# A two-stream transformer kernel: low-rank rows made and turned as two items, and smaller gates for a stage's last eight experts

## What is computed

```python
def _mla_kv(ckv, kr, lp, ang):            # keys and values through a rank of 128
    kv = _rmsnorm(ckv, lp["kv_norm_g"]) @ lp["w_ukv"]
    ...
def _mla_q(cq, lp, ang):                  # queries through a rank of 256
    q = _rmsnorm(cq, lp["q_norm_g"]) @ lp["w_uq"]
    ...
def _peer(h, w_pq, peer_keys, peer_down, peer_up):
    # 8 heads x top 16 of 128x128 experts: 128 experts for each token
    ...
    a = einsum("tkd,td->tk", peer_down[ee], hh)
    act = gg * gelu(a)
    return einsum("tk,tkd->td", act, peer_up[ee])
for l in range(DEPTH):
    m_x = _modulation(c, w_mod[l], b_mod[l])
    mix_x, _ = _token_mix(modulated(x), lp, ang, kv_c)
    x = x + m_x[2] * mix_x
    x = x + m_x[5] * _peer(modulated(x), ...)
    # in layer 0 the same for the context; in layer 1 only its keys and values
```

## Time and profile before

| what | us |
| --- | --- |
| median of three runs | 4265.7 |
| lowest and highest | 4264.2, 4265.86 |
| the profiled execution | 4267.86 |
| its span in the trace | 4266.6 |

### The profile page before, as it was taken

One profiled execution on the slowest core, in us unless ns is written; L12 is line 12 of the kernel. 1 busy time (PEld: TensorE's weight loads), 2 busy tenths in 40 slices (PEclk: granted clock), 3 DMA queues, 4 the chain that ended last, 5 costly groups with the idle time before them and its releaser, 6 DMA issues. The chain is left out here.

```text
span 4266.6 us, 41116 instructions
## 1 busy us (share of the span) xinstructions
PE 3701.3 (87%) x14648; PEld 2615.9 (61%) x14648; DVE 2319.3 (54%) x5440; ACT 658.8 (15%) x1794; POOL 1307.3 (31%) x1125
## 2 busy tenths in 40 slices
PE   8988899998998689999988998767778899878777
PEld 6667787886857578888846884333334787333332
DVE  3331011457658766766752126767774123877774
ACT  2232100110001220000002111111112211111111
POOL 1000000000755446665630003434442001544442
PEclk9999999999999889999999999988999999999989
DMA  8652344433998779999961349979996326999997
GB/s 321 237 202 106 117 151 155 153 117 136 413 383 305 263 255 381 406 399 385 409 247 51 143 167 364 414 311 380 409 412 283 109 105 249 402 419 420 419 414 320
DMA packets 207819, 1208.67 MB, mean 283 GB/s; under 512 B 23696, under 2 KB 24848, under 8 KB 96000
## 3 DMA queue, kind: packets, MB, share of 16 engines
q0 software_dynamic: 154368, 855.71, 50.1%
q1 hardware_dynamic: 53248, 350.32, 21.6%
HBM read 1204.79 MB, written 1.15 MB: 283 GB/s over the span
## 5 line engine op out<-in xcount | busy, mean ns | idle before, releaser
L1222 PE MATMUL bank<-big 128*128 128x256 f32 (+3 forms) x9848 | 2142.1, 378 | 65.4 <-issue 16.8
L1222 PEld LDWEIGHTS bank<-big 128*128 128x128 f32 x9848 | 1834.9, 191 | 375.1 <-issue 85.0
L2406 POOL DMA_INDIRECT big<-in_pboth,big x1024 | 1240.6, 1211 | 1243.0 <-PE bank L1609 651.3
L1609 PE MATMUL bank<-big 128*128 128x512 f32 x2048 | 1009.4, 651 | 304.2 <-ACT big L2370 304.1
L2087 DVE CUSTOM_DVE_ANT_0 big<-big 128x1024 f32<-128x1024 f32 x768 | 926.5, 1223 | 346.8 <-DMA big<-in_pboth,big 336.1
L1609 PEld LDWEIGHTS bank<-big 128*128 128x128 f32 x2048 | 416.4, 208 | 894.3 <-issue 500.0
L2393 POOL TENSOR_TENSOR big<-big 128x1 f32<-128x1 f32 (+1 forms) x49 | 40.9, 834 | 1553.7 <-DVE big L1663 1553.6
L2098 DVE SCALAR_TENSOR_TENSOR big<-big 128x1024 f32<-128x1024 f32 x254 | 326.1, 1284 | 34.8 <-DMA big<-in_pboth,big 11.9
L2370 ACT ACTIVATE big<-big 128x128 f32<-128x128 f32 x512 | 164.7, 391 | 258.6 <-DVE big L2066 251.9
L1257 PE MATMUL bank<-big 128*128 128x128 f32 x596 | 95.9, 297 | 74.2 <-ACT big L2172 23.6
L2360 ACT ACTIVATE big<-big 128x4 f32<-128x4 f32 x128 | 26.4, 206 | 785.3 <-DVE big L2062 785.3
(11 more groups left out here) (203 smaller groups left out, 2191.2 us busy)
## 6 DMA issues: line engine op xcount, KB each, us to landing
big<-in_w SPq DMA_DIRECT2D x104, 1024.0 KB
big<-in_wmod POOLq DMA_DIRECT2D x48, 1024.0 KB, 8.4
big<-in_wgu SPq DMA_DIRECT2D x44, 1024.0 KB
big<-in_wzg SPq DMA_DIRECT2D x36, 1024.0 KB, 4.8
big<-in_wro SPq DMA_DIRECT2D x32, 1024.0 KB
big<-in_wpq SPq DMA_DIRECT2D x24, 1024.0 KB, 4.9
big<-in_wd SPq DMA_DIRECT2D x22, 1024.0 KB
big<-in_pboth,big POOLq DMA_INDIRECT x1024, 18.5
```

The source lines that it names most:

```text
L1222: last = pe.matmul(o, a, b, start=(i == 0), stop=(i == n - 1))
L1609: last = pe.matmul(u.ap, d.ap, row[:, 512 * i:512 * i + 512], start=(k == 0), stop=(k == 127))
L2406: g.indirect_dma_start(out=s.ap, out_offset=None, in_=table, in_offset=bass.IndirectOffsetOnAxis(ap=index, axis=0)).then_inc(s.full[0], 16)
```

## The change

Three edits. First, `low_rank` becomes two items: `low_rank` (product, squares, root) and `low_turn` (turning and taking from PSUM). `mixer` now emits the product of keys and values with the rope key, then the product of the queries, then the turning and `kv_up` of the keys, then the turning and `q_up` of the queries. Loads follow in the order `wkv`, `wcq`, `wukv`, `wuq`. Second, the eight matmuls of `keep_busy` in front of each turning of the x stream are gone. Third, the gates of the last eight experts of a stage (second block of tokens, experts 120 to 127) hold 2, 2, 2, 1 and 1 experts where they held 4 and 4. With the first edit the yields change: `keys_values` hands back 6, 1 and 6 units where it handed 7 and 7, the queries' product 7 and their turning 2 where there was none, so that a mixer's stream stands 8 units later from there on, the context's too; and the side generator takes three steps for keys and values in place of two.

```diff
-    def low_rank(self, banks, sm, ws, wt, hT, ready, n, tmp, dst, gcols):
+    def low_rank(self, banks, sm, ws, wt, hT, ready, n, tmp):
         u = banks.take()
         r = self.rstd(sm, 2, 1.0 / n, EPS)
+        scaled = [self.tick("lowrank_rows"), u.free]
+        self.put("low_rank", ws=ws, wt=wt, hT=hT, ready=ready, n=n, u=u, tmp=tmp, r=r, scaled=scaled)
+        return u.full, scaled
+
+    def low_turn(self, banks, sm, n, tmp, dst, gcols, scaled):
         parts = [banks.take() for _ in range(2)]
-                 warm=8 if sm is self.small else 0,
-                 scaled=[self.tick("lowrank_rows"), u.free])
-        return parts[1]
+        self.put("low_turn", n=n, tmp=tmp, dst=dst, gcols=gcols, parts=parts, scaled=scaled)
+        return parts[1].free
...
-        low = self.low_rank(banks, sm, [w], wt, hT, hT_ok, P, ckn, ckvT, self.col[l, "kvg"])
+        _, scaled = self.low_rank(banks, sm, [w], wt, hT, hT_ok, P, ckn)
...
-        yield
+        yield 6
+        turned = self.low_turn(banks, sm, P, ckn, ckvT, self.col[l, "kvg"], scaled)
+        yield 1
         w = self.load(wr, t["wukv"][l], 1024)
...
-        yield
+        yield 6
         return [r, ku[3].free, vu[1].free]
...
-        kv_ok = yield from self.keys_values(banks, wr, sm, ar, l, hT, hT_ok, K, Vv, cs)
-        if rope_on and l == 1:
-            kv_ok += self.ctx_kv_ok
+        kv = self.keys_values(banks, wr, sm, ar, l, hT, hT_ok, K, Vv, cs)
+        yield next(kv)
...
+        made, scaled = self.low_rank(banks, sm, [w], w.ap.rearrange("p (k n) -> p k n", k=8), hT, None, 256, cqn)
+        w.free(made)
+        yield
+        kv_ok = yield from kv
+        if rope_on and l == 1:
+            kv_ok += self.ctx_kv_ok
+        turned = self.low_turn(banks, sm, 256, cqn, cqT, self.col[l, "qg"], scaled)
+        yield 2
         w = self.load(wr, t["wuq"][l], 1536)
...
+        ends = {(tt, k) for tt, k in steps if k % 4 == 3} | {(1, k) for k in (121, 125, 126)}
+        at = 0
         for n, (tt, k) in enumerate(steps):
...
-            if k % 4 == 3:
+            if (tt, k) in ends:
...
-                a, c = act[:, tt, k - 3:k + 1], 4 * (n // 4 % 8)
-                args = dict(at=a, u=gl[:, c:c + 4], ag=ag[:, c:c + 4], tanh=tick("gelu_tanh"))
-                put("gelu", gat=gat[:, tt, k - 3:k + 1], cubed=tick("gelu_cubed"), **args)
+                m = len(batch)
+                at = 0 if at + m > 32 else at
+                mine = slice(k + 1 - m, k + 1)
+                args = dict(at=act[:, tt, mine], u=gl[:, at:at + m], ag=ag[:, at:at + m], tanh=tick("gelu_tanh"))
+                put("gelu", gat=gat[:, tt, mine], cubed=tick("gelu_cubed"), **args)
+                at += m
...
-            if tt == 0:
-                keep_busy(v, warm)
```

More of the change, by code:

```diff
@@ L779, in keys_values @@
         w.free(vu[1].full)
-        put("kv_up", ws=[w], ckvT=ckvT, K=K, Vv=Vv, ku=ku, vu=vu, ready=low.free)
-        yield
+        put("kv_up", ws=[w], ckvT=ckvT, K=K, Vv=Vv, ku=ku, vu=vu, ready=turned)
+        yield 6
         return [r, ku[3].free, vu[1].free]
@@ L818, in mixer @@
             q_ok = tick("q_turned") if rope_on else u.free
-            put("q_up", ws=[w] if h == 0 else [], w_ok=w.full, wq=wq, cqT=cqT, Q=Q[:, h:h + 2, :], h=h, u=u, ready=low.free,
+            put("q_up", ws=[w] if h == 0 else [], w_ok=w.full, wq=wq, cqT=cqT, Q=Q[:, h:h + 2, :], h=h, u=u, ready=turned,
                 u2=banks.take() if rope_on else None, cs=cs, rt=rt, done=q_ok)
@@ L1451, in col_turn, with low_rank @@
             turn(u, [h[:, (4 * g + i) * P:(4 * g + i + 1) * P] for i in range(4)]).then_inc(u.full[0], 1)
-    def low_rank(ws, wt, hT, ready, n, u, tmp, parts, scaled, warm, **_):
+    def low_rank(ws, wt, hT, ready, n, u, **_):
         opened(u)
@@ L1458, in low_rank, with low_turn @@
         tokens_first(pe, u, wt, hT, n=n).then_inc(u.full[0], 1)
+    def low_turn(n, tmp, parts, scaled, **_):
         for tt, v in enumerate(parts):
             opened(v)
-            if tt == 0:
-                keep_busy(v, warm)
             pe.wait_ge(*scaled[tt])
@@ L1618, in tensor_program @@
                  branch_gate=branch_gate, branch_out=branch_out, mix_out=mix_out, ffn_in=ffn_in, ffn_out=ffn_out, ffn_last=ffn_last, mod=mod,
-                 mod_columns=mod_columns, col_turn=col_turn, low_rank=low_rank, key_rope=key_rope, key_roped=key_roped, kv_up=kv_up, q_up=q_up,
-                 att_score=att_score, att_turnp=att_turnp, att_out=att_out, att_turn=att_turn, fourier=fourier, pool=pool,
+                 mod_columns=mod_columns, col_turn=col_turn, low_rank=low_rank, low_turn=low_turn, key_rope=key_rope, key_roped=key_roped,
+                 kv_up=kv_up, q_up=q_up, att_score=att_score, att_turnp=att_turnp, att_out=att_out, att_turn=att_turn, fourier=fourier, pool=pool,
                  token_gate=token_gate, mix=mix, token_out=token_out, peer_q=peer_q, peer_scores=peer_scores, up_pe=up_pe)
@@ L1900, in col_turn, with low_rank, low_turn @@
         i.then_inc(u.free[0], 1)
-    def low_rank(n, dst, gcols, r, parts, **_):
+    def low_rank(r, **_):
         spread(r)
+    def low_turn(n, dst, gcols, parts, **_):
         for tt, u in enumerate(parts):
@@ L2134, in vector_program @@
                  context_in=context_in, mod_add=mod_add, mod_gain=mod_gain, mod_row=mod_row, mod_zero=mod_zero,
[L2135 removed]
+                 mod_columns=mod_columns, row_scale_v=row_scale_v, col_turn=col_turn, low_rank=low_rank, low_turn=low_turn, key_roped=key_roped, kv_up=kv_up,
                  q_up=q_up, load_cs=load_cs, att_score=att_score, fourier=fourier, pool=pool, mix=mix, token_out=token_out,
```

5 lines of the change are left out of this document (removed).

## The result

The changed kernel took 4254.42 us in the median of 13 runs (4245.61 to 4262.41); the kernel before, run beside it, 4264.43 (4257.22 to 4271.8). The ratio is 0.9975 with a 95% interval of 0.9965 to 0.9984: 10.0 us faster, between 7 and 15. The prediction was -18.3 us, that is 4247.4, and a range from 4237 to 4260: the direction holds and the time lies in the range, but only somewhat more than half of the forecast size came. The profiled executions differ by less, 4267.86 before and 4262.41 after, since the latter is one of the slowest of its 13; so the places are compared by their own lengths, and with the traces of the experiments as repetitions.

What follows compares the result with a forecast made beforehand. PE, busy 87% of the span, was taken as the main bound, with gathers, hand-overs and DVE limiting places. Terms -9.6 + 0.8 - 6.8 - 7.1 + 3.4 + 2 - 1 + 0 = -18.3 gave 4247.4 us, range 4237 to 4260.

Steps and rivals of the forecast that it cites:

- The low-rank part of x: Keys' product to first `q_up` in x's mixers: 29.44 us falls to 24.66, -4.8 per layer, -9.6 for both.
- +0.8 for the clock: Layer 0's keys' product: a slower PE start after slightly longer idle time without the removed matmuls, +0.8 us.
- The clock, rival (c): x's low-rank parts: without the removed matmuls PE stays at 1.2 GHz, work doubles, +42 us, 4289 us; chance 0.04.
- Stage ends: Last experts of both stages: smaller gates let PE finish 3.4 us earlier per stage, -6.8 for both.
- The load queue: End of the context's mixer: PE's 8.22 us wait at 739.28 for a `w1` chunk falls to about 1.1, -7.1.
- Junction: Streams' junction at 2206: more context work on DVE delays the row for `peer_add`, net +3.4 us, bounds +1 to +6.
- Ranking: Merge of x's first mixer output with the context's ranking, 940 to 1031: more DVE instructions, +2 us, bounds -5 to +4.
- The context's low-rank part: Context's mixer: waits covered, but taking the keys falls behind the first block's decays on DVE; -1 us, bounds -4 to +3.
- Side generator: Context's keys and values among layer 0's experts: stalls move, copies' stall 10 to 13 us; 0 taken, bounds -5 to +7.
- Rival (a): The `w1` wait at 739 stays or comes back: sum -11.2, 4254.5 us; chance 0.18.
- Rival (b): Shifted context stream gives more back, junction +6, ranking +4, side generator +7: -6.7, 4259 us; chance 0.15.

Runs made afterwards that it cites:

- e2: The full change with the last experts' gates back at 4 and 4, so the low-rank edits and removed matmuls alone: 4261.86 us, ratio 0.9986 to the kernel before.
- e3: The full change with fewer units handed back, so the two streams merge as before, without the shift: 4255.4 us, ratio 0.9975 to the kernel before.
- e1: The kernel before with only the smaller gates (2, 2, 2, 1, 1) for a stage's last eight experts: 4260.42 us, ratio 0.9987 to the kernel before.
- e6: The kernel before with only gates of 4, 2, 1, 1 for a stage's last eight experts: 4262.74 us, ratio 0.9996 to the kernel before.
- e7: The kernel before with only the eight `keep_busy` matmuls before each turning taken out: 4268.43 us, ratio 1.0009 to the kernel before.
- e4: The full change with the eight `keep_busy` matmuls kept before the first turning of each rank in x: 4264.81 us, ratio 0.9996 to the kernel before.
- e9: The kernel before with only the context's stream moved by 8 units, the shift alone: 4269.62 us, ratio 1.0007 to the kernel before.
- e5: The kernel before with only the loads of `iota` and keys put one `w1` chunk later in SP's list: 4254.09 us, ratio 0.9973 to the kernel before.
- e8: The kernel before with x's new order without `keep_busy`, context keys before queries unshifted, late `iota` and keys loads, gates 2, 2, 1, 1, 1, 1: 4245.08 us, ratio 0.9956.

## Why the prediction was right, and where its size was off

The time lies in the range and the direction held. Of the forecast's -18.3 us some 8 did not come: mostly the two streams, for which the sum of the load queue, the junction, the ranking and the context's part was -2.7 and which gave +2 to +6 up to x's modulated rows at 2230, and partly the stage ends. By the steps of the prediction:

- **The low-rank part of x** (-9.6, with +0.8 for the clock: -8.8). Right, and a little too small: about 6.8 in layer 0 and 3.8 in layer 1, 10.6 us together by e2, e3 and the full change against the five kernels in the old order. In layer 0 the two profiled executions give 4.7 us up to `q_up` (30.81 and 26.08), as forecast; the further 2 us were not in the sum. The granted clock of that whole part was 0.94 before and 0.95 after (0.95 in e1 too), so the +0.8 for a slower start isn't seen there; in layer 1 it went from 0.99 to 0.98. The waits that come back were foreseen with their places. Layer 1's shortfall (-3.4 to `q_up` in the two profiled executions instead of -4.8) is the slower clock in the two first products; in e1 and e6, where the keys' product of the old order met the same clock, the old stretch was 1.6 us longer too, and the difference is 5.0.
- **The clock, rival (c).** It didn't decide, but its mechanism is real and was shown in e7: without the matmuls and without the new order the part gets 5.4 us slower. I had them down as filler on the path; in the old order they stood in waiting time and held the clock up.
- **Stage ends** (-6.8). The mechanism was right, to 0.1 us where the clock stayed up (6.44 measured, 9.84 - 3.4 = 6.4 forecast), the size was off where the clock fell: -1.6 and -1.7 in the profiled execution, -2.9 and -1.7 in e1, -2.9 and -3.4 in e3 and e4. I had reckoned a duration at full clock with no slack behind it. With gates of four a batch that ran at the lower level mostly ended in the 1.2 to 2.8 us of idle time ahead of the next, and moved the end in one stage of ten (e9); packed without a gap, it moved the end in six of the eight stages with gates of 2, 2, 2, 1, 1. Their mean is 7.3 us, 2.5 less than the 9.84 of before. e1 as a whole gave -5.3.
- **The load queue** (-7.1). The wait went, whole and not down to 1.1 us, and with the chunk at full clock it was 10 rather than 8 us: e5. The step that failed is "the gain is passed on". It is, if only the loads move (e5: -10.3 at 1623). With the shift of the streams it is lost again between 1030 and 1623 us, 4.6 + 8.0 = 12.6 us (e9). I had looked at the shift at single places, and for the stretch from 1031 to 1623 I had no term at all, though PE waits often for DVE in it.
- **Junction** (+3.4): +2.5, the same in the four kernels with the shift (22.9 to 23.1 us against 20.2 to 20.5 without).
- **Ranking** (+2): between the third and the eighth taking (L1809) PE's idle time went from 10.9 to 12.4 us and the length from 52.4 to 54.0, +1.5. A window at fixed times doesn't show it, since its work isn't the same (136 matmuls of PE where the earlier trace rows has 117):

```profile
980.00:1020.00 40.00, 31.16 (x136) 26.74 (x136) 33.08 (x123) 2.30 (x3) 0.67 (x1) 0.88 0.26 97
```

- **The context's low-rank part** (-1): +3 by e3 at 1030 us, at the upper bound. The turned rows are taken behind the first block's decays: a wait of 4.0 us at 353 in e3, for the queries, and of 3.8 us at 332 in e8, for the keys. In e9 and the full change x has the same lead, so that with the shift this cost doesn't show.
- **Side generator** (0): the root's stall is still 13.53 us, the turning makes one of 1.94 where 4 to 5 were forecast, and the copies' stall of 9.24 has become 12.35, within the 10 to 13 forecast. DVE's idle time from the first to the last inner product of the stage grew by 1.5 us, from 217.9 to 219.4. From the first residual sum of layer 0's mixer (L1977) to the last inner product it is 769.6 us in the mean of the six kernels without the edit (766.2 to 771.3) and 770.6 of the five with it (766.2 to 773.4): it can't be told from nothing. Rows of the full change:

```profile
2858.53 0.17 DVE L1678 TENSOR_SCALAR big<-big 128x2 f32<-128x2 f32 x1 [13.53 <-ACT big L2173]
...
2881.88 0.49 DVE L1923 TENSOR_TENSOR big<-bank,big 128x128 f32<-128x128 f32 x2 [1.94 <-PE bank L1272]
...
2919.29 0.69 DVE L1945 COPY big<-bank 128x512 f32<-128x512 f32 x1 [12.35 <-PE bank L1504]
```

Rival (a) named the size of the result (4254.5) for another reason than the true one: the wait for a `w1` chunk did not come back. Of its kind there is only one wait of 2.9 us for a `wzg` load at 521, in the full change and in e9, where 0.9 us for `wro` stood before. Rival (b), that the shift gives its gain back, was the right idea at the wrong places.

With the measured terms: -10.6 for the low-rank part, -3.3 to -6.3 for the stage ends, and for the shift up to x's modulated rows of layer 0 +2.2 against e1 and +6.2 against the kernel before (+4.3 between the means of four kernels each) make -8 to -15; -10.0 was measured, with an interval from -7 to -15.

## What to carry to other kernels

A merge of two streams is a whole: if an edit moves one stream against the other, price every stretch behind it in which the two share a waiting engine, or move only the one transfer that matters; here the latter alone gave as much as the whole change. Filler matmuls that stand mostly in waiting time cost little and may hold the clock up, so take them out only together with the edit that puts work in their place. And where a tail is packed until it has no slack, reckon with the slower clock for part of it.

## What the runs showed of the hardware

Executions of one and the same order agree to 0.3 us over long stretches: from 1030 to 1623 us 592.6 to 592.8 us in five kernels with before's order there (before, e1, e5, e6, e7), and 605.2 in the four with the shift. How such a stretch divides can differ: up to 1263 and behind it 232.4 and 360.3 us in the kernel before, 231.7 and 360.9 in e6, 230.0 to 230.2 and 362.5 to 362.6 in e1, e5 and e7. Behind 1623 they agree less: up to the second half of x's modulated rows the same order took 603.8 us in before, 604.2 in e7, 607.2 in e5, 607.5 in e1 and 607.6 in e6. Row gathers run in both stretches (1058 to 2214 us), so they alone don't explain it; the cause stays open. A single trace can be off by 4 us there. The first comparison of two profiles, +10.4 us between 1263 and 1623, was partly the other effect, the division at 1263: the kernel before took 360.3 us where most of its repetitions took 362.5.

Full and lower clock could be read from the same matmuls: the experts' matmuls at the end of layer 1 took 7.14 us for 16 at full clock, and 8.84 in the full change, where the granted clock was down for a part:

```profile
4240.00:4250.00 10.00, 8.11 (x15) 0.83 0.03 11
```

The idle time ahead of the latter was 1.90 us, shorter than the 2.82 us after which a batch of the kernel before still ran at full speed; in e9 a batch behind 2.83 us ran slowly. The length of one wait alone doesn't tell whether the next work runs slowly.
